# Late layers of a three-layer block: the halves of the rotary embedding exchanged by DMA instead of by a product, latent keys in two products instead of four

## The reference

```python
h = rms_norm(x, g_norm)
z = jnp.einsum('bsd,dc->bsc', h, w_in)
aq, ak, av, ag, bq, bk, bv, bg, cq, ckv, ckr, cg = jnp.split(z, idx, axis=-1)

qa = rms_norm(aq.reshape(bsz, s_len, A_HEADS, HEAD_DIM), a_qn)
ka = rms_norm(ak.reshape(bsz, s_len, A_KV_HEADS, HEAD_DIM), a_kn)
qa = apply_axial_rope(qa, axial_row, axial_col)      # two rotations of 32 features each
ka = apply_axial_rope(ka, axial_row, axial_col)
oa = dense_gqa_blocks(qa, ka, va, HEAD_DIM ** -0.5) * jax.nn.silu(ag)

qb = apply_rope(bq..., rope_1d[0], rope_1d[1])       # one rotation of 64 features
kb = apply_rope(bk..., rope_1d[0], rope_1d[1])
ob = windowed_sink_gqa(qb, kb, vb, b_sink, HEAD_DIM ** -0.5) * jax.nn.silu(bg)

qc = jnp.einsum('bsr,rc->bsc', rms_norm(cq, c_qn), c_wuq)...
kv = jnp.einsum('bsr,rc->bsc', rms_norm(ckv, c_kvn), c_wukv)...   # latent keys and values
...
return x + jnp.einsum('bsm,md->bsd', o, w_out)

def apply_rope(x, cos, sin):
    x1, x2 = jnp.split(x, 2, axis=-1)
    rot = jnp.concatenate([-x2, x1], axis=-1)
    return x * cos + rot * sin
```

## Time and profile before

| | |
|---|---|
| median of three runs | 1826.12 us (1824.75 to 1828.1) |
| the profiled execution | 1826.74 us, span in the trace 1825.0 us |
| PE busy | 1765.7 us (97% of the span) |
| DVE, ACT, POOL busy | 801.9 us (44%), 723.6 us (40%), 604.0 us (33%) |
| granted TensorE clock | 0.988 of full speed on average |

### The profile page before, as it was taken

The page is one execution under the profiler, slowest core; times in us unless marked ns, Lnnn a source line. Parts: engine busy times, 40 slices in busy tenths (PEclk is TensorE's granted clock), DMA queues, the critical chain, the costliest instruction groups (busy, mean ns, idle before and its releaser), DMA issues.

```text
span 1825.0 us, 25256 instructions
## 1 busy us (share of the span) xinstructions
PE 1765.7 (97%) x10862; PEld 1390.1 (76%) x10862; DVE 801.9 (44%) x1342; ACT 723.6 (40%) x1228; POOL 604.0 (33%) x182
## 2 busy tenths in 40 slices
PE   8999999999999999998999999989999999999997
PEld 5778899988888888877888888877684478776456
DVE  8756646623123121114670143145446654526653
ACT  5656665433233332233331222234426533345541
POOL 3534210333333434432454444424332114333112
PEclk9999999999999999998999999989999999999998
DMA  5121200326223323222222232213220012211001
GB/s 205 70 93 24 72 3 25 132 70 191 79 95 104 123 70 110 96 93 69 93 92 93 97 111 93 92 70 140 70 83 10 1 48 97 93 69 47 1 1 47
DMA packets 37504, 144.71 MB, mean 79 GB/s; under 512 B 3155, under 2 KB 15835, under 8 KB 23696
## 3 DMA queue, kind: packets, MB, share of 16 engines
q1 hardware_dynamic: 18944, 121.53, 18.8%
q10 hardware_dynamic: 18448, 21.57, 3.9%
HBM read 140.93 MB, written 5.30 MB: 80 GB/s over the span
## 4 chain that ended last, share of the span: by engine, by line
PE 87%; DVE 5%; ACT 4%; issue 1%; DMA 1%; ACTq 0%; POOL 0%; SPq 0%; POOLq 0%; DVEq 0%
PE bank L407 56%; PE bank L1145 6%; PE bank L613 5%; PE bank L418 4%; PE bank L2196 3%; PE bank L2220 3%; PE bank L2203 2%; DVE WK L978 1%; PE bank L1653 1%; PE bank L1629 1%; PE bank L2149 1%; ACT WK L2330 1%; ACT w_part L365 1%; PE bank L2228 1%; DMA WK<-wgate 1%
## 5 line engine op out<-in xcount | busy, mean ns | idle before, releaser
L407 PE MATMUL bank<-x_part,w_part 128*128 128x512 f32 x3216 | 746.8, 392 | 1.5 <-ACT WK L2309 0.8
L407 PEld LDWEIGHTS bank<-x_part,w_part 128*128 128x128 f32 x3216 | 601.0, 188 | 135.4 <-issue 10.7
L2660 POOL TENSOR_TENSOR w_part<-RAW,w_part 128x2048 fp32r<-128x2048 f32 (+1 forms) x90 | 404.2, 4493 | 678.4 <-ACT w_part L365 678.4
L365 ACT ACTIVATE w_part<-RAW 128x2048 fp32r<-128x2048 f32 (+1 forms) x90 | 165.8, 1842 | 175.5 <-PE bank L407 138.0
L2660 POOL TENSOR_TENSOR w_part<-WK,w_part 128x2048 fp32r<-128x2048 f32 (+1 forms) x30 | 123.7, 4124 | 246.9 <-ACT w_part L365 246.9
L407 PE MATMUL bank<-f_part,w_part 128*128 128x512 f32 x768 | 174.4, 389 | 0.0
L407 PEld LDWEIGHTS bank<-f_part,w_part 128*128 128x128 f32 x768 | 144.1, 188 | 29.9
L1145 PE MATMUL bank<-WK 64*64 64x64 f32 (+1 forms) x1456 | 103.4, 249 | 4.8 <-ACT WK L1311 2.5
L1145 PEld LDWEIGHTS bank<-WK 64*64 64x64 f32 (+1 forms) x1456 | 99.0, 163 | 7.3 <-ACT WK L1311 2.6
L978 DVE SCALAR_TENSOR_TENSOR WK<-bank,COL,WK 128x510 f32<-128x510 f32 (+1 forms) x96 | 71.7, 749 | 48.6 <-ACT WK L920 45.9
L2677 POOL TENSOR_TENSOR WK<-BASE,WK 128x1024 f32<-128x1024 f32 x16 | 30.4, 1898 | 167.5 <-DVE WK L2503 167.5
(11 more groups left out here) (286 smaller groups left out, 2236.1 us busy)
## 6 DMA issues: line engine op xcount, KB each, us to landing
RAW<-wts SPq DMA_DIRECT2D x83, 1024.0 KB, 4.8
WK<-wts SPq DMA_DIRECT2D x23, 1024.0 KB, 4.8
WK<-scratch ACTq DMA_DIRECT2D x16, 256.0 KB, 2.7
WK<-decay_rows ACTq DMA_DIRECT2D x14, 256.0 KB, 6.6
RAW<-wts SPq DMA_DIRECT2D x7, 512.0 KB, 3.5
WK<-wts SPq DMA_DIRECT2D x7, 512.0 KB, 3.4
scratch<-bias_rows ACTq DMA_DIRECT2D x4, 768.0 KB, 8.8
WK<-xT SPq DMA_DIRECT2D x4, 512.0 KB, 7.3
```

The source lines that it names most:

```text
L365: act.eng.activation(high_part(i), raw_part(i), ACT.Copy).then_inc(*act.did(("hi", i)))
L407: mm = pe.eng.matmul(b[:, :], W[w][:, k, c:c + P], src[x][k], start=start and k == 0 and n == 0, stop=stop and k == kn - 1 and n == 2)
L2660: eng.tensor_tensor(low_part(i), raw_part(i), high_part(i).bitcast(F32), ALU.subtract).then_inc(w_split, 1)
```

## The change

The feature order of group A's heads is changed on the host (`HALVES`), in the weights, the norm gains and the tables, so that in both groups the half to be exchanged with partitions 0 to 31 of a head lies in its partitions 32 to 63. The sign goes into the sine tables. The eight products per layer with the swapping matrix go. In their place ACT's queue issues, for the tiles of A and for those of B, four DMAs each (`exchange`) that copy 32 partitions of `QKF` to the neighbouring 32 partitions of a second buffer `XCH`, 256 KB each (32 partitions by 8 KB), where the memory of the gates is free at that time. `rope` on DVE reads `XCH` in SBUF in place of the product in PSUM, and C's scalings now stand between the ropes: `ccp` 0 behind rope 1, `ccp` 1 behind rope 3, `ccp` 2 behind rope 5. `csq` on ACT no longer waits for the last rope. The keys from the latent vector are two products of 128 columns in place of four of 64; ACT's four copies stay.

```diff
@@ lay_pe
             fm((L, "B", 3), f"L{l}B", 3 * P, HTS)
-            pe.wait_ge(*at(("tabs", l)))
             pe.wait_ge(*at(("small", l)))
-            for i in range(8):
-                pe.wait_ge(*at((L, "qn", i)))
-                b = job((L, "rot", i))
-                E.matmul(b[:, :], tab("ra") if i < 4 else tab("rb"), QKF[:, i, :], start=True, stop=True).then_inc(...)
             for i in range(3):
                 fm((L, "C", i), f"L{l}C", i * P, HTS)
...
-            for h in range(4):
-                b = job((L, "uk", h))
-                E.matmul(b[0:64, :], UKV[:, h * 64:(h + 1) * 64], CL[:, 2, :], start=True, stop=True).then_inc(...)
+            for j in range(2):
+                b = job((L, "uk", j))
+                E.matmul(b[:, :], UKV[:, j * P:(j + 1) * P], CL[:, 2, :], start=True, stop=True).then_inc(...)
@@ lay_act
+            def exchange(k):
+
+                act.wait_ge(*at(("pe", (L, "sum", 0))))
+                for i in range(4 * k, 4 * k + 4):
+                    act.wait_ge(*at((L, "qn", i)))
+                for b in range(4):
+                    frm = b ^ 1
+                    A.dma_start(XCH[32 * b:32 * b + 32, 4 * k:4 * k + 4, :], QKF[32 * frm:32 * frm + 32, 4 * k:4 * k + 4, :])\
+                        .then_inc(turned_in[l][k], 16)
+
             ahead(f"L{l}B", 0)
+            exchange(0)
+            exchange(1)
             ahead(f"L{l}B", 2 * P)
 
             for i, m in enumerate((P, 64, P)):
-                act.wait_ge(*at((L, "ropes")))
                 act.wait_ge(*at((L, "ccp", i)))
                 A.activation(SQL[0:m, i, :], CL[0:m, i, :], ACT.Square).then_inc(*act.did((L, "csq", i)))
                 if i == 1:
                     ahead(f"L{l}C", 0)
@@ lay_dve
-            def rope(dst, rot, c, s, tmp, m, rel, lab):
-
-                dve.wait_ge(*at(("pe", rot)))
-                V.tensor_tensor(tmp[0:m], ps(rot)[0:m, :], s[0:m], ALU.mult).then_inc(*dve.did(free=rot))
-                V.tensor_tensor(dst[0:m], dst[0:m], c[0:m], ALU.mult).then_inc(*dve.did())
-                dve.wait_ge(*dve.last())
-                V.tensor_tensor(dst[0:m], dst[0:m], tmp[0:m], ALU.add).then_inc(*dve.did(*lab))
+            def rope(i):
+
+                k = i // 4
+                x, y = QKF[:, i, :], XCH[:, i, :]
+                dve.wait_ge(*at(("turned", l, k)))
+                V.tensor_tensor(y, y, tab(("asn", "bs")[k]), ALU.mult).then_inc(*dve.did())
+                V.tensor_tensor(x, x, tab(("ac", "bc")[k]), ALU.mult).then_inc(*dve.did())
+                dve.wait_ge(*dve.last())
+                V.tensor_tensor(x, x, y, ALU.add).then_inc(*dve.did())
...
             for i in range(8):
-                rope(QKF[:, i, :], (L, "rot", i), ...)
-            for i in range(3):
-                scaled(CL[:, i, :], (L, "C", i), P, (L, "ccp", i))
+                rope(i)
+                if i % 2 and i < 7:
+                    scaled(CL[:, i // 2, :], (L, "C", i // 2), P, (L, "ccp", i // 2))
```

More of the change, by code:

```diff
@@ L50 @@
 TURNED = [*range(16, 32), *range(16)]
+HALVES = [*range(16), *range(32, 48), *range(16, 32), *range(48, 64)]
 MIXED = [12, 13, 6, 9, 0, 3, 14, 15, 7, 10, 1, 4, 8, 11, 2, 5]
@@ L117, in rope_tables @@
     return np.cos(ang).T.astype(np.float32), np.sin(ang).T.astype(np.float32)
[L120 to L129, removed]
 def shape_constants():
@@ L150, in shape_constants @@
     for n in range(2):
-        ax = np.concatenate([axr[n], axc[n]], 0)
+        ax = np.concatenate([axr[n], axc[n]], 0)[HALVES]
         tabs.append(np.concatenate([ax, ax], 0))
@@ L154, in shape_constants @@
         tabs.append(np.concatenate([one_d[n], one_d[n]], 0))
+    for x in (tabs[1], tabs[3]):
+        x[0:32] *= -1.0
+        x[64:96] *= -1.0
     for n in range(2):
@@ L160, in shape_constants @@
         tabs.append(x)
-    tabs += [half_turn(P, 32), half_turn(P, 64)]
     k = np.arange(3 * P)[None, :]
@@ L168 @@
 TAB = dict(ac=(0, 512), asn=(512, 512), bc=(1024, 512), bs=(1536, 512), cc=(2048, 512), cs=(2560, 512),
-           ra=(3072, 128), rb=(3200, 128), win=(3328, 384))
-NTAB = 3712
+           win=(3072, 384))
+NTAB = 3456
 NGDN = 7 * P + 64
@@ L320, in build @@
         bias_in = [sem(f"bias_in{i}") for i in range(2)]
+        turned_in = [[sem(f"{k}_halves_exchanged{l}") for k in "ab"] for l in range(LAYERS)]
         out_done = sem("out_done")
@@ L323, in build @@
         rows_in = [sem(f"decay_rows_in{u}") for u in range(8)]
-        for s in [rows_out, bias_rows_out, *rows_in, *w_in_slot, w_split, const_in, gdnc_in, wgate_in, sel_in, *x_in, x_again, tabs_in, *small_in, *bias_out, *bias_in, out_done]:
+        for s in [rows_out, bias_rows_out, *rows_in, *w_in_slot, w_split, const_in, gdnc_in, wgate_in, sel_in, *x_in, x_again, tabs_in, *small_in, *bias_out, *bias_in, *turned_in[0], *turned_in[1], out_done]:
             byname[s.name] = s
@@ L341, in build @@
             table[("small", l)] = (small_in[l], 16)
+            for k in range(2):
+                table[("turned", l, k)] = (turned_in[l][k], 64)
         def weights(chunk, c):
@@ L2069, in build @@
         GTM = wk(25600, KO, S)
+        XCH = GTM
         MIX = parts("mix_part", 15360, KO, S)
@@ L2143, in lay_pe @@
             fm((L, "B", 3), f"L{l}B", 3 * P, HTS)
-            pe.wait_ge(*at(("tabs", l)))
             pe.wait_ge(*at(("small", l)))
-            for i in range(8):
-                pe.wait_ge(*at((L, "qn", i)))
-                b = job((L, "rot", i))
-                E.matmul(b[:, :], tab("ra") if i < 4 else tab("rb"), QKF[:, i, :], start=True, stop=True).then_inc(*pe.did(("pe", (L, "rot", i))))
             for i in range(3):
@@ L2174, in lay_pe @@
                 E.matmul(b[:, :], UQ[0:64, 1, h * P:(h + 1) * P], CL[0:64, 1, :], start=False, stop=True).then_inc(*pe.did(("pe", (L, "uq", h))))
-            for h in range(4):
-                b = job((L, "uk", h))
-                E.matmul(b[0:64, :], UKV[:, h * 64:(h + 1) * 64], CL[:, 2, :], start=True, stop=True).then_inc(*pe.did(("pe", (L, "uk", h))))
+            for j in range(2):
+                b = job((L, "uk", j))
+                E.matmul(b[:, :], UKV[:, j * P:(j + 1) * P], CL[:, 2, :], start=True, stop=True).then_inc(*pe.did(("pe", (L, "uk", j))))
             gates(0)
@@ L2307, in lay_act @@
             for h in range(4):
-                act.wait_ge(*at(("pe", (L, "uk", h))))
-                A.activation(CK[0:64, h, :], ps((L, "uk", h))[0:64, :], ACT.Copy).then_inc(*act.did(*([(L, "kready")] if h == 3 else []), free=(L, "uk", h)))
+                j, o = divmod(h, 2)
+                act.wait_ge(*at(("pe", (L, "uk", j))))
+                A.activation(CK[0:64, h, :], ps((L, "uk", j))[64 * o:64 * o + 64, :], ACT.Copy)\
+                    .then_inc(*act.did(*([(L, "kready")] if h == 3 else []), free=(L, "uk", j) if o else None))
             for g in range(2):
@@ L2429, in lay_dve @@
             for i in range(8):
-                rope(QKF[:, i, :], (L, "rot", i), tab("ac" if i < 4 else "bc"), tab("asn" if i < 4 else "bs"), SQL[:, i % 4, :], P, None,
-                     [(L, "ropes")] if i == 7 else [])
-            for i in range(3):
-                scaled(CL[:, i, :], (L, "C", i), P, (L, "ccp", i))
+                rope(i)
+                if i % 2 and i < 7:
+                    scaled(CL[:, i // 2, :], (L, "C", i // 2), P, (L, "ccp", i // 2))
             for i, m in enumerate((P, 64, P)):
@@ L2731, in part @@
         w = w2[l][:, SPLIT2[n]:SPLIT2[n] + width]
+        if n in ("aq", "ak"):
+            w = w.reshape(D, width // 64, 64)[:, :, HALVES].reshape(D, width)
         return w if order is None else np.concatenate([w[:, h * 64:h * 64 + 64] for h in order], 1)
@@ L2775, in lay_out @@
     put("norm_a", A(norm_a)[0][:, None])
-    put("aqn", np.concatenate([A(a_q_norm_2)] * 2, 1).T)
-    put("akn", np.concatenate([A(a_k_norm_2)] * 2, 1).T)
+    put("aqn", np.concatenate([A(a_q_norm_2)[:, HALVES]] * 2, 1).T)
+    put("akn", np.concatenate([A(a_k_norm_2)[:, HALVES]] * 2, 1).T)
     cq = np.zeros((P, 4), np.float32)
```

## The result

| | before | after |
|---|---|---|
| median, four runs each | 1825.43 us (1823.88 to 1828.10) | 1836.94 us (1836.07 to 1837.72) |
| ratio after to before | | 1.0068, 95% interval 1.0056 to 1.0080 |
| span of the profiled execution | 1825.0 us | 1835.9 us |
| PE busy | 1765.7 us | 1755.1 us |

What follows compares the result with a forecast made beforehand. TensorE was taken to bound the kernel (87% of the last chain). Two layers at +1.3 - 1.8 us and the 0.77 us wait gave -1.8 us, a median of 1824.3 us, range 1817 to 1831.

Steps and rivals of the forecast that it cites:

- What bounds the kernel, what is removed: TensorE holds 87% of the last chain; 6.47 us of rotations and 1.8 of keys go per layer, 0.77 once.
- Two SBUF operands exclude POOL: DVE rope steps reading two SBUF tiles and POOL's low parts exclude each other for whole instructions, 4.5 us in rope 5.
- the DMA issues on ACT: Eight issues on ACT's queue take 3.4 us, moving V's rounding behind them from 1565.14 to 1568.6.
- The landing: A's exchange lands after 7.6 us, at 1572.9, ahead of POOL's end at 1575.1, so POOL decides the first rope.
- As one load of 1 MB: A's four queued copies land like one 1 MB load, 4.8 us, plus 2.8 for the weight load's traffic.
- The idle time and the clock: TensorE idles 6.2 us ahead of `css`, the clock halves, and `uq` starts 1.3 us later than before.
- The price of 1.6: Half the work of the 3 us or little more after the idle time ahead of `css`, lost to the clock.
- Sum: Per layer +1.3 - 1.8 = -0.5 us; twice, and the first layer's 0.77: -1.8 us.
- The rivals: No or brief POOL collision, 1810.8 us (0.13); clock stays up, 1822.6 (0.12); exchange lands late, to 1835.5 (0.25).
- The slower one: A's exchange lands after 1575.1, each us late delaying `css` by 1 us per layer; up to 1835.5 us, chance 0.25.
- The edit at nothing: Ten fewer products shift later banks; the second layer's first tile waits 0.9 us for a residual, hidden by `x_part`.

Runs made afterwards that it cites:

- V's rounding first: The changed kernel with ACT's rounding of V's weights ahead of the eight DMA issues instead of behind them; 1830.45 us, 1.0025 to the kernel before.
- the kernel with G0 late too: The changed kernel with the exchange on SP's queue ahead of the weight load and both roundings of G0's weights behind C's norm factors; 1806.66 us.
- the filler: The changed kernel with 44 unused products put where TensorE idles ahead of `css`; 1831.52 us, 1.0038 to the kernel before.
- both edits together: The changed kernel with V's rounding ahead of the DMA issues and both roundings of G0's weights behind C's norm factors; 1822.48 us.

## Why the prediction was wrong

- *What bounds the kernel, what is removed.* Right: PE lost the rotations and the keys. The keys saved 2.15 per layer, predicted 1.8 (the faster pace of the rotations, 1.95, was nearer), and the 0.77 of the earlier trace rows went.
- *Two SBUF operands exclude POOL.* Right in the places, the number and the size: the first rope, rope 5 and rope 7 with 4.8 to 4.9 us each. `ccp` 2 begins 8.6 behind `ccp` 1 (1593.62 to 1602.25 on DVE), predicted 8.8. The Trainium skill's rule (SBUF — State Buffer, "Who interferes with whom") and the trace agree.
- **The step that failed: the DMA issues on ACT.** The sum took 3.4 us for eight, from two issues with nothing queued; they took 8.2. Its bounds, 3.0 to 3.9, were far too narrow. They came from one pair of rows, though the trace of before has eight issues in a row on the same queue, at 181.24, that take 8.0 us, and four at 0.6 each elsewhere. V's rounding came 5.4 us late (4.8 of it the issues, the rest a later start), V's low part with it, and the ropes ran freely 5.4 us later than predicted. `css` is 5.2 late for it, in the first layer 4.8. Behind V's rounding, or on SP, the issues no longer held up the ropes (6.5 us in the two layers, shown).
- *The landing.* 10.6 and 11.6 us after the first issue, predicted 7.6, bounds 4.0 to 13.6. It had no effect on the changed kernel, since POOL still ended later. But with the issues as cheap as predicted it would have decided: with V's rounding first the ropes start at 21.6 and not at 19.0. "As one load of 1 MB" was wrong: with no weight load beside it, only B's exchange behind it, it takes 6.9 to 8.3 (6.9 from 1552.38 to 1559.30 in the kernel with G0 late too), and the load adds 3.3 to 4.5.
- *The idle time and the clock.* 11.7 us instead of 6.2, so the clock was down for the whole of `css`. From `css` to `uq` it took 11.8 in the second layer and 13.3 in the first, predicted 10.3, before 8.7: a further 1.5 and 3.0. Right in kind, and the filler shows that it costs. The price of 1.6 came from 3 us of products at half pace behind the gap of the earlier trace rows. Here the clock stayed down for some 6 us of products in the second layer and 9 in the first. In the stretch of the earlier trace rows it also stood at 0.50 already ahead of the gap (from 1214 on), so those rows don't show that a gap of 3.7 us brings it down.
- *Sum.* In the second layer -0.5 was predicted and +5.8 found: 5.2 from the late ropes, 1.5 from the clock, less 0.4 from the keys. In the first, -1.3 and +6.0: 4.8, 3.0, less 0.4. These are 6.3 and some 7.3 us; less the 0.95 by which the rest of this execution was shorter it is 12.7, the distance from the predicted span, 1823.2, to the measured one, 1835.9.
- *The rivals.* The slower one was a late exchange, with POOL's end as the point from which it decides. The kernel was slower by the same chain, but what came late was POOL's end itself. I had treated that as fixed to half a microsecond, and so the range ended 6 us short.
- *The edit at nothing.* The later banks did shift: PE now waits for the last residual, 0.88 us, and the end of the first tile hides it.

```profile
1520.87 11.16 PE L401 MATMUL bank<-x_part,w_part 128*128 128x512 f32 x48 [0.88 <-DVE WK L2552]
```

What stays open: why the later ones of eight DMAs in a row take 1 us and more to issue when the first take 0.5, and how long a copy inside SBUF takes when nothing runs beside it, as no run has one alone. What the clock costs is known from the filler alone, 3.8 us in the first layer and 1.4 to 3.0 in the second.

## What to carry to other kernels

Work taken off the bounding engine is worth what the next wait on that engine lets through; follow the chain that replaces it with every instruction that stands behind a new one on its queue, DMA issues too. An issue behind which a rounding, a scaling or a table waits belongs on another queue, or behind that work, and a large load beside a short copy that is waited for belongs behind it. When an operand moves from PSUM to SBUF, look for GpSimd instructions that run at the same time, and move those to where nobody waits.

## What the runs showed of the hardware

- Eight DMAs of 256 KB issued in a row hold their queue for 7.3 to 8.8 us, on ACT as on SP, from DRAM as inside SBUF (0.37 to 2.44 each). Two of 1 MB take 0.5 each. The Trainium skill calls the time to initiate a DMA usually small relative to the DMA itself (DMA: Bandwidth & Descriptors, "Issuing engines are not separate DMA queues"). For one DMA the trace agrees, 1.0 us against a landing of 8.1. But the eight issues together were as long as one landing, and what stands behind them on the queue waits for all of them. That DMAs interleave on the same DMA engines whichever engine issued them, as that section says, agrees too: A's exchange lands 11.2 and 11.6 us after its first issue on SP behind the load, and 10.6 to 12.2 on ACT.
- The four copies of 256 KB of one exchange land 6.9 to 8.3 us after the first issue with no load beside them and 10.6 to 12.2 beside a load of 1 MB, which itself lands after 6.5 to 7.4 instead of 4.8.
- After 9 to 12 us without products the granted clock was 0.50 for `css` and its neighbours. After 5 us of idle time `css` ran at the same half pace (2.04 and 2.07 a pair with both edits together). The Trainium skill has TensorE go to 1.2 GHz when idle and back with activity (TensorE: Matmul & The Clock Gate, "Part 1: The HAM clock gate"); the rows agree.
